# Two fused transformer blocks on one core: the opening of the latent attention in another order

## The reference

```
h = rms_norm(x, mix_pre_norm)
proj = h @ w_in
gq, gk, gv, gg, ga, gb, cq, ckv, kr = split(proj)
# gated delta rule group
q, k, v = split(silu(causal_conv4(concat(gq, gk, gv))))
q, k = l2_norm(q) * 128 ** -0.5, l2_norm(k)
log_a = -exp(a_log) * softplus(ga + dt_bias)
g = cumsum(log_a) within chunks of 64 tokens
o_gdn = gated_delta_rule(q, k, v, sigmoid(gb), log_a)   # uses exp(g), exp(g_last - g), exp(g_last)
# latent attention group: 8 heads, 64 + 32 features in a query and a key, 64 in a value
q = rms_norm(cq) @ w_q_up             # 256 latents
kv = rms_norm(ckv) @ w_kv_up          # 128 latents: keys and values
q_rope, k_rope = rotate(q_rope), rotate(kr)   # one k_rope for all heads
o_mla = softmax(mask(q @ k.T * 96 ** -0.5)) @ v
x = x + rms_norm(concat(o_gdn, o_mla) @ w_out)
x = x + rms_norm(square(relu(rms_norm(x) @ w_up)) @ w_down)
```

## Time and profile before

| | |
|---|---|
| time, median of 3 runs | 3049.79 us (3043.07 to 3052.67) |
| profiled execution: time, span | 3050.98 us, 3049.0 us |
| busy: PE, DVE, POOL, ACT | 2891.5, 1590.9, 1053.1, 740.8 us |
| chain that ended last | PE 84%, DVE 6%, POOL 4%, ACT 3%, issue 2%, DMA 1% |
| TensorE's mean granted clock | 0.977 of full speed |

### The profile page before, as it was taken

How to read it: one execution, slowest core, us unless ns; L and a number is a source line. 1 busy time by engine, 2 the same in 40 slices (tenths; PEclk the granted TensorE clock), 3 DMA queues, 4 the chain that set the end, 5 groups by cost and what they waited for, 6 DMA issues and landing times.

```text
span 3049.0 us, 42703 instructions
## 1 busy us (share of the span) xinstructions
PE 2891.5 (95%) x16394; PEld 2327.4 (76%) x16394; DVE 1590.9 (52%) x1925; ACT 740.8 (24%) x1486; POOL 1053.1 (35%) x738
## 2 busy tenths in 40 slices
PE   7998898979899999999899999989998999999998
PEld 6886567868788888888678887657876888888886
DVE  3464554661677777777742004674144455445446
ACT  3323564333311011101420004553134001100111
POOL 4321001347533334333542322212368233323332
PEclk9998999999999999999899999999999999999999
DMA  3210000004222222223221111001132111111111
GB/s 123 56 28 11 10 6 23 3 25 143 75 85 87 81 84 83 76 83 88 90 63 45 52 35 35 22 1 49 50 136 62 49 42 54 48 48 41 55 48 62
DMA packets 213437, 172.15 MB, mean 56 GB/s; under 512 B 15544, under 2 KB 188879, under 8 KB 213327
## 3 DMA queue, kind: packets, MB, share of 16 engines
q1 hardware_dynamic: 160670, 135.47, 14.4%
q10 hardware_dynamic: 52656, 35.13, 3.8%
HBM read 162.19 MB, written 8.39 MB: 56 GB/s over the span
## 4 chain that ended last, share of the span: by engine, by line
PE 84%; DVE 6%; POOL 4%; ACT 3%; issue 2%; DMA 1%; SPq 0%; POOLq 0%; DVEq 0%; ACTq 0%
PE ps L921 13%; PE ps L923 12%; PE ps L922 12%; PE ps L1338 8%; PE ps L1339 7%; PE ps L1340 7%; PE ps L1130 2%; PE ps L1048 2%; PE ps L940 1%; PE ps L942 1%; PE ps L941 1%; PE ps L1070 1%; PE ps L1276 1%; PE ps L1521 1%; POOL rstd L721 1%
## 5 line engine op out<-in xcount | busy, mean ns | idle before, releaser
L292 POOL TENSOR_SCALAR slab_hi<-raw 128x1024 fp32r<-128x1024 f32 (+1 forms) x236 | 268.3, 1137 | 1512.7 <-PE ps L923 565.2
L295 POOL TENSOR_TENSOR slab_lo<-raw,slab_hi 128x1024 fp32r<-128x1024 f32 (+1 forms) x236 | 580.6, 2460 | 19.7
L921 PE MATMUL ps<-act_hi,slab_hi 128*128 128x512 f32 x1472 | 577.0, 392 | 5.7 <-DVE act_lo L2092 3.9
L923 PE MATMUL ps<-act_hi,slab_lo 128*128 128x512 f32 x1472 | 574.6, 390 | 0.0
L922 PE MATMUL ps<-act_lo,slab_hi 128*128 128x512 f32 x1472 | 574.2, 390 | 0.0
L2490 DVE TENSOR_TENSOR acc<-ps,acc 128x512 f32<-128x512 f32 x512 | 339.9, 687 | 214.0 <-PE ps L1340 213.8
L1338 PE MATMUL ps<-slab_hi,hid_hi 128*128 128x512 f32 x1024 | 405.3, 396 | 11.3 <-DVE hid_lo L2481 8.9
L1339 PE MATMUL ps<-slab_hi,hid_lo 128*128 128x512 f32 x1024 | 401.6, 392 | 0.0
L1340 PE MATMUL ps<-slab_lo,hid_hi 128*128 128x512 f32 x1024 | 400.9, 391 | 0.0
L1895 ACT ACTIVATE relu<-ps 128x512 f32<-128x512 f32 x128 | 77.3, 604 | 1038.7 <-PE ps L923 1014.9
L921 PEld LDWEIGHTS ps<-act_hi,slab_hi 128*128 128x128 f32 x1472 | 277.6, 189 | 63.9 <-issue 3.2
(11 more groups left out here) (319 smaller groups left out, 4215.3 us busy)
## 6 DMA issues: line engine op xcount, KB each, us to landing
raw<-in_w_in SPq DMA_DIRECT2D x56, 512.0 KB, 3.9
w_ada<-in_w_ada ACTq DMA_DIRECT2D x48, 512.0 KB, 4.1
raw<-in_w_out SPq DMA_DIRECT2D x32, 512.0 KB, 3.6
raw<-in_w_up SPq DMA_DIRECT2D x32, 512.0 KB, 4.1
raw<-in_w_down SPq DMA_DIRECT2D x32, 512.0 KB, 3.5
raw<-in_w_mlp_in SPq DMA_DIRECT2D x32, 512.0 KB, 4.1
raw<-in_w_mlp_out SPq DMA_DIRECT2D x32, 512.0 KB, 3.5
x_tok<-in_x SPq DMA_DIRECT2D x8, 512.0 KB, 6.1
```

The costliest lines, as they stand in the source:

```text
L292: pool.tensor_scalar(self.hi[s][:, 0:width], self.raw[r][:, 0:width], 1.0, 0.0, ALU.mult, ALU.add)\
L295: pool.tensor_tensor(self.lo[s][:, 0:width], self.raw[r][:, 0:width], self.hi[s][:, 0:width].bitcast(F32), ALU.subtract).then_inc(self.spl ...
L921: pe.matmul(o, hi[:, w], a_hi[:, k, cols], start=(k == 0), stop=False)
L923: mm = pe.matmul(o, lo[:, w], a_hi[:, k, cols], start=False, stop=(k == nk - 1))
```

## The change

- On all engines the last three of the 12 conv panels are written out behind a loop of nine.
- **Decay sums** stand on TensorE before panel 9 (three matmuls) and behind it (one), all into bank 7; ScalarE's copies and exponentials stand behind its panels 8 and 9, VectorE's difference before panel 9.
- **Sums of squares**: VectorE's copy from bank 6 stands behind tap 0 of the same panel, with its wait for TensorE, instead of behind the silu. The square of panel 11 is left out. POOL makes the norms as soon as the sums of the k heads are there.
- **Latents**: turned in the order `LAT_GROUPS` (both query halves of the first 512 tokens first). ScalarE takes the six out ahead of the last panel's tanh; VectorE rotates the key between the last panel's taps and its silu.
- **Projections of pair 0** come before the **values**; each waits for the latents that it reads and goes to a bank that they have left. The values go to `V_BANKS`, each with its own wait. The first scores wait for 4 value copies, the next ones for all 8.
- **Key buffers**: the copy into pair 1's second buffer moves into pair 0, step 5; `q_feat` and `k_feat` of the first heads move to other space, so that they don't lie on `conv_y` and `conv_t`.
- **SP**: pair 0's weights are asked for behind panel 10, `w_kv` behind panel 11.

The diff, cut to its core:

```diff
-MLA_FIRST_BANKS = (7, 6, 5, 4, 3, 1)
+MLA_FIRST_BANKS = (7, 0, 1, 2, 3, 6)
+MLA_FIRST_FEATS = (2, 4, 4, 4, 5, 6)
+LAT_GROUPS = ((0, 0), (1, 0), (0, 1), (1, 1), (2, 0), (2, 1), (3, 0), (3, 1))
 LAT_BANKS = (7, 0, 1, 2, 3, 6, 4, 5)
+V_BANKS = (4, 5, 7, 0, 1, 2, 3, 6)
...
-            R2.panel_done(sp, 0, GDN_PANELS - 1)
+            R2.panel_done(sp, 0, GDN_PANELS - 2)
             w_q_up = d["w_q_up"][0].rearrange("(k p) n -> p k n", p=P)
-            sp.dma_start(w_kv[:], d["w_kv_up"][0]).then_inc(sem("w_kv_in"), 16)
             half = ROPE // 2
             for i in range(MLA_PAIRS):
+                if i == 1:
+                    R2.panel_done(sp, 0, GDN_PANELS - 1)
+                    sp.dma_start(w_kv[:], d["w_kv_up"][0]).then_inc(sem("w_kv_in"), 16)
...
-            pool.wait_ge(sem("ss_gdn_done"), GDN_PANELS + 2)
+            pool.wait_ge(sem("ss_gdn_done"), 2 * GDN_HEADS + 3)
...
+            with pe.Fori(0, GDN_PANELS // 3 - 1) as i:
                 for j in range(3):
...
+                    gdn_panel(i, j)
...
+            decay_sum(0, C_ONES, slice(0, CHUNK))
+            decay_sum(1, C_CSUM, slice(0, P))
+            decay_sum(2, C_CHUNK, slice(0, P)).then_inc(sem("cumsum_prod"), 1)
+            gdn_panel(GDN_PANELS // 3 - 1, 0)
+            pe.wait_ge(sem("e_last_done"), 1)
+            pe.wait_ge(sem("cumsum_done"), 2)
+            decay_sum(3, C_ONES, slice(CHUNK, P)).then_inc(sem("cumsum_prod"), 1)
+            for j in range(1, 3):
+                gdn_panel(GDN_PANELS // 3 - 1, j)
...
-            pe.wait_ge(sem("mla_k_rope_done"), 2)
             for n in range(MLA_CHUNKS):
+                pe.wait_ge(sem("lat_feat_done"), MLA_FIRST_FEATS[n])
                 mla_project(0, n)
+
+            pe.wait_ge(sem("w_kv_in"), 16)
+            w_v = w_kv[:].rearrange("p (h c) -> p h c", c=P)[:, :, NOPE:P]
+            for t, b in enumerate(V_BANKS):
+                name, count = (("mla_k_rope_done", 1), ("mla_k_rope_done", 1), ("proj_read", 3), ("proj_read", 5),
+                               ("mla_rope_done", 1), ("mla_rope_done", 2), ("proj_read", 7), ("proj_read", 9))[t]
+                pe.wait_ge(sem(name), count)
+                pe.matmul(ps[:, b, :].rearrange("p (h e) -> p h e", e=V_DIM), ckv_f[:, t * P:(t + 1) * P], w_v,
+                          start=True, stop=True).then_inc(sem("v_prod"), 1)
+
+            pe.wait_ge(sem("v_done"), 4)
             mla_scores(0, 0)
+            pe.wait_ge(sem("v_done"), NT)
...
+                if last:
+                    for n in range(6):
+                        kind, h = LAT_GROUPS[n]
+                        dst = (cq_f[:, 0, :], cq_f[:, 1, :], ckv_f[:])[kind][:, h * HALF:(h + 1) * HALF]
+                        gain = V_QN + kind if kind < 2 else V_KVN
+                        act.wait_ge(sem("lat_turned"), n + 1)
+                        act.activation(dst, ps[:, LAT_BANKS[n], :], ACT.Copy, scale=vec[:, gain:gain + 1])\
+                            .then_inc(sem("lat_feat_done"), 1)
...
+                ch.link(dve.tensor_scalar(conv_y[:], xpad[:, 0:SEQ], tap(0), None, ALU.mult))
+                dve.wait_ge(sem("ss_prod"), p + 1)
+                dve.tensor_copy(ss_gdn[:, :, p], ps[:, 6, 0:NT]).then_inc(sem("ss_gdn_done"), 1)
...
+                if isinstance(i, int) and j == 2:
+                    key_rotation()
+                dve.wait_ge(sem("conv_tanh_done"), p + 1)
...
+                    if i == 0 and s == 5:
+                        dve.wait_ge(sem("v_prod"), NT)
+                        dve.tensor_copy(k_f[1][1][rr, :], k_f[0][0][rr, :]).then_inc(sem("mla_k_rope_done"), 1)
```

More of the change, by code:

```diff
@@ L965, in _, with gdn_panel @@
             pe.wait_ge(sem("lat_done"), NT)
-            with pe.Fori(0, GDN_PANELS // 3) as i:
-                for j in range(3):
-                    p = 3 * i + j
-                    R2.ready(pe, 3 * i, j)
-                    pe.wait_ge(sem("conv_in_done"), p + 1)
-                    b = 2 * j
-                    panel(R2.hi[j], R2.lo[j], in_hi, in_lo, (b, b + 1), KD, (sem("panel_half"), R2.used))
-                    pe.wait_ge(sem("conv_sq_done"), p + 1)
-                    pe.wait_ge(sem("ss_gdn_done"), p + 2)
-                    for t in range(NT):
-                        mm = pe.matmul(ps[:, 6, t:t + 1], conv_t[:, t * P:(t + 1) * P], ones[:, 0:1],
-                                       start=True, stop=True)
-                    mm.then_inc(sem("ss_prod"), 1)
+            def gdn_panel(i, j):
+                p = 3 * i + j
+                R2.ready(pe, 3 * i, j)
+                pe.wait_ge(sem("conv_in_done"), p + 1)
+                b = 2 * j
+                panel(R2.hi[j], R2.lo[j], in_hi, in_lo, (b, b + 1), KD, (sem("panel_half"), R2.used))
+                pe.wait_ge(sem("conv_sq_done"), p + 1)
+                pe.wait_ge(sem("ss_gdn_done"), p + 2)
+                for t in range(NT):
+                    mm = pe.matmul(ps[:, 6, t:t + 1], conv_t[:, t * P:(t + 1) * P], ones[:, 0:1],
+                                   start=True, stop=True)
+                mm.then_inc(sem("ss_prod"), 1)
@@ new lines, in _, with decay_sum @@
+            with pe.Fori(0, GDN_PANELS // 3 - 1) as i:
+                for j in range(3):
+                    gdn_panel(i, j)
+            pe.wait_ge(sem("log_a_done"), 1)
+            n_gh = NT * GDN_HEADS
+            la = g_la[:].rearrange("p t h -> p (t h)")
+            def decay_sum(n, lhs, rows):
+                return pe.matmul(ps[:, 7, n * n_gh:(n + 1) * n_gh], consts[rows, lhs:lhs + P], la[rows, :], start=True, stop=True)
+            decay_sum(0, C_ONES, slice(0, CHUNK))
+            decay_sum(1, C_CSUM, slice(0, P))
@@ L984, in _ @@
+            for (kind, h), b in zip(LAT_GROUPS, LAT_BANKS):
                 c0, m = ((LAT_CQ, P), (LAT_CQ + P, P), (LAT_CKV, P), (LAT_KR - ROPE, 3 * ROPE))[kind]
@@ L1754, in _ @@
                 mla_take(0, n)
+            for t, b in enumerate(V_BANKS):
+                act.wait_ge(sem("v_prod"), t + 1)
+                act.copy(v_t[:, t, :, :].rearrange("p h e -> p (h e)"), ps[:, b, :]).then_inc(sem("v_done"), 1)
             for i in range(MLA_PAIRS):
@@ L2176, in _ @@
+            with dve.Fori(0, GDN_PANELS // 3 - 1) as i:
                 ch.loop(i, 9)
                 for j in range(3):
[L2178 to L2191 removed]
@@ L2209, in _ @@
-            dve.wait_ge(sem("mla_k_rope_done"), 1)
-            dve.tensor_copy(k_f[0][1][rr, :], k_f[0][0][rr, :]).then_inc(sem("mla_k_rope_done"), 1)
+                    conv_panel(i, j)
+                ch.end(GDN_PANELS // 3 - 1)
             dve.wait_ge(sem("cumsum_done"), 2)
             dve.tensor_tensor(g_ekd[:], g_tot[:], g_cum[:], ALU.subtract).then_inc(sem("g_tail_done"), 1)
+            for j in range(3):
+                conv_panel(GDN_PANELS // 3 - 1, j)
             scale = float(DQK) ** -0.5
```

135 lines of the change are left out of this document (56 added, 79 removed).

## The result

| | before | after |
|---|---|---|
| time, median (runs) | 3047.45 us (3043.07 to 3052.67, 5) | 3026.64 us (3023.87 to 3030.78, 5) |
| ratio, 95% interval | | 0.9929 (0.9918 to 0.9941) |
| profiled execution: time, span | 3050.98, 3049.0 us | 3029.37, 3027.6 us |
| busy: PE, DVE, POOL, ACT | 2891.5, 1590.9, 1053.1, 740.8 us | 2881.4, 1591.0, 1052.5, 737.9 us |
| mean granted clock | 0.977 | 0.983 |

The change is 0.7% faster, 20.8 us between the medians and 21.6 between the profiled executions. The same kernel beside a later experiment had the ratio 0.9927 (0.9913 to 0.9941).

What follows compares the result with a forecast made beforehand. TensorE, busy nearly everywhere, was taken as the bound, losing time to waits and a lower clock in the opening. Terms 22.5 + 2.7 - 0.7 = 24.5 us took 3050.98 to 3026.5, in median terms 3025 us; range 3014 to 3040.

Steps and rivals of the forecast that it cites:

- Decay sums: Four small matmuls moved from behind the values to around conv panel 9, pushing everything behind them by 0.95 us.
- The copy in the taps: VectorE's sum-of-squares copy behind tap 0: costs about 0.4 us per conv panel, removes the 4.5 us wait for bank 6.
- rival C: Wait between conv taps closes a ring through ScalarE and lengthens panels: slower, 3060 us at a 5 us wait; chance 0.04.
- Transposes: The 32 latent transposes in the opening run through in one piece of 3.8 us, 273.63 to 277.4 us.
- Projections of pair 0: Run on TensorE from 277.4 to 286.0 us, covered by weight loads issued about 12 us sooner.
- Values: Value matmuls from 286.0 to 292.9 us, VectorE's second query rotation ending 0.2 us before the sixth needs it.
- Pair 1: Its first projection starts at 293.9 or 294.0 us instead of 316.54, 22.5 us sooner.
- The clock behind the wait: Pair 1's first two chunks regain the upper clock: 2.7 us gained, ends 0 and 2.7.
- The key copy: Moved into pair 0 at step 5, where TensorE waits for an exponential: costs 0.7 us, ends 0 and 0.7.
- Rival A: TensorE's clock stays low in the new opening: only 9 us gained, 3041 us; chance 0.09.
- Rival B: The 24.5 us become a wait in a later stage, on a transfer or POOL: 3050 us; chance 0.06.

Runs made afterwards that it cites:

- experiment 10: Changed kernel with the cumulative decay sum computed seven times instead of once behind panel 8's small matmuls; ratio 0.9939 against the kernel before, three runs.
- experiment 1: Kernel before with only VectorE's sum-of-squares copy moved behind tap 0 in every conv panel; median 3044.4 us, ratio 0.9991.
- experiment 5: Changed kernel with pair 0's weights again asked for behind the last conv panel and the value weights; ratio 0.9947 against the kernel before.
- Experiment 2: Kernel before with unused fp32 matmuls added where TensorE stood idle in the opening, no wait taken away; ratio 0.9969.
- experiment 6: Changed kernel with pair 0's key copy at step 3 instead of 5, second scores waiting for seven value copies; ratio 0.9923 against the kernel before.
- experiment 3: Changed kernel with the last conv panel's sum-of-squares copy put back behind that panel's taps; ratio 0.9940 against the kernel before.
- experiment 4: Changed kernel with the old order put back, values ahead of pair 0's projections; ratio 0.9963 against the kernel before.

## Why the prediction was right, by its steps

Forecast 3025 us in the range of 3014 to 3040; measured 3026.64. The sum said 24.5 us sooner behind pair 0's exponential; the profile has 24.47. That the two agree to the tenth is luck: pair 1 came 22.1 us sooner instead of 22.5, and the scores between its first two chunks, 0.60 us instead of 1.06, gave back as much and were in no term. In the total the gain was smaller than the sum: 20.8 us between the medians, 22 by the ratio, for 24.5. The kernel before had the median 3047.45 in the five runs instead of the 3049.79 from which the forecast counts, and that brought the times themselves nearer to each other. Step by step:

1. *Decay sums*: 0.95 us forecast, 1.3 measured (pitches 13.58 and 13.16 for 12.73). The term took their length behind the values; between large matmuls the same eight records take 0.81 and 0.34 us from start to start, and some 0.1 us more is lost around them. That they could set off a low clock (experiment 10) was in no term.
2. *The copy in the taps*: the pitch stayed 12.73; rival C fell. The 4.5 us were gone, but not because bank 6 alone was free: in experiment 1 the copy by itself starts the values 0.6 us sooner behind T, with 8.8 us of waiting ahead of them for 8.0. The step credited the copy with what the whole of the reordering earns.
3. *Transposes*: at 274.30 for 273.63 (0.3 more from step 1, 0.3 from the start of the conv stage), then 3.5 us in one piece, as forecast (3.8).
4. *Projections*: 277.83 to 286.4 for 277.4 to 286.0. The cover by the earlier weights was real, and without it 3.3 us of wait and 1.8 of clock (experiment 5).
5. *Values*: to 293.28 for 292.9. VectorE's second rotation ended at 290.3 for 290.1, its scales at 293.06 for 292.8. "Just covered, by 0.2 us" was the boldest line, and it held: no wait in front of the sixth value.
6. *Pair 1*: 294.44 for 293.9 to 294.0, that is 22.1 us sooner for 22.5. All of the difference is the later T.
7. *The clock behind the wait*: both chunks at 1.88 us, 2.7 us as forecast. But this term was only a part of what the clock gave: terms 3, 4 and 5 had been worked out at the upper rate, so another 6 us of clock (transposes 1.3, values 3.1, projections 1.8) hid inside the 22.5. Experiment 2 puts the clock's part at 9.5 us, on the kernel before.
8. *The key copy*: the exponential's wait is 1.93 for 1.22, exactly the 0.7 us, and experiment 6 gives them back.

Rival A fell. It had the rule of the Trainium skill, page "TensorE: Matmul & The Clock Gate", section "A second HAM failure mode: psum-queue depth-cycling", which tells of a bf16 kernel. In this opening, in float32, the rows speak against it: eight value banks one after the other, and scores behind pauses of 0.45 us, at 1.00 in every profile of the changed kernel; also with 1.6 us of standing (experiment 3). What lowered the clock between T and P was 3.3 us and more of standing (0.73 in experiment 5, 0.71 in experiment 4). Shorter waits do it at times: behind the 1.9 us in front of X the window of 310 to 330 us has 0.91 in experiments 3 to 5, and 1.00 in the changed kernel. And at the second conv panel, at about 143 us, records of 0.63 us follow waits of only 0.31 us (experiment 6) and 0.46 us (experiment 10); so the length of the wait before them does not decide alone, and what else does stays open. One reading of the prediction was wrong here: it took the window of 292.5 to 298.2 us for values with a pause in front of each bank. The values of before are one row without a pause; what stands in that window are the waits of 0.77 and 0.55 us on ScalarE behind them. It was no witness against the rule, and the verdict on A rests on the profiles after.

Rival B is not shown and not shut out: the profiled execution lost 3 of its 24.5 us by the end. The second profile of the same kernel, with the same opening to 0.1 us, has a span of 3022.0 instead of 3027.6, so one pair of profiles can't tell such a loss from where later stages happened to fall; the two ratios (0.9929 and 0.9927, about 22 us) leave room for a loss of 2 us.

## What to carry to other kernels

Price a wait by its length and by the slow records behind it; here the second was two fifths of the whole. Where waits stand in a row, follow each to the last thing that its releaser needs (a square, a buffer that lies on another), since taking one of 4.5 us away alone brought the next block only 0.6 us forward; look at the clock too, which in that run gave more than the wait (5.7 us at X, with no less standing). And of two blocks with the same length put that one first whose results feed the slower engine and the next load: here this order was worth 9 us for no work saved.

## What had not been expected of the hardware

- Work without use made the kernel faster by 0.3%: 13.6 us of float32 matmuls in waits kept the clock at 1.00. It did not pay at the conv panels, where the next wait ended no sooner and the time came back as a longer wait.
- The granted clock can fall while TensorE never stands: 18 records of small matmuls instead of 6, behind sixteen with one column each, and the clock was 0.68 in the next 5 us (one profile).
